# The triangular solve of a recurrent mixer in blocks of 8 with Horner steps, and decays as exponentials of scanned logarithms

## What is computed

```python
g = sigmoid(z @ g1) @ g2
kk = heads(k * k_k); kk = kk * rsqrt(sum(kk * kk) + 1e-12)
for d in range(2):                      # forward and backward in time
    w_log = -softplus(-(w0[d] + tanh(z @ w1[d]) @ w2[d])) - 0.5
    decay = exp(-exp(w_log))            # = exp(-exp(-0.5) * sigmoid(...))
    a = sigmoid(a0[d] + (z @ a1[d]) @ a2[d])
    kd = heads(k * (1 + (a - 1) * k_a))
    # scan over the 256 positions, one 64x64 state per head:
    #   sa    = state @ (-kk_t)
    #   state = state * decay_t + sa (x) (kk_t * a_t) + v_t (x) kd_t
    #   y_t   = state @ r_t
```

## Time and profile before

| | us |
|---|---|
| median of 3 runs | 3765.77 (3765.65 to 3765.84) |
| the profiled execution, its own time | 3762.42 |
| its span, from the first to the last instruction | 3760.6 |

### The profile page before, as it was taken

One profiled execution on the slowest core, in us unless ns is written; L12 is line 12 of the kernel. 1 busy time (PEld: TensorE's weight loads), 2 busy tenths in 40 slices (PEclk: granted clock), 3 DMA queues, 4 the chain that ended last, 5 costly groups with the idle time before them and its releaser, 6 DMA issues. The chain is left out here.

```text
span 3760.6 us, 63506 instructions
## 1 busy us (share of the span) xinstructions
PE 3675.8 (98%) x26848; PEld 3401.5 (90%) x26848; DVE 2378.3 (63%) x4235; ACT 424.9 (11%) x1010; POOL 1169.8 (31%) x926
## 2 busy tenths in 40 slices
PE   7999999999999999999989999999999999999998
PEld 6778885999999999999977888859999999999998
DVE  7986853894688654444389867539946885444442
ACT  1014211100111000000010232111101110000000
POOL 3610000033333355554245100001333334554552
PEclk9999999999999999999999999999999999999999
DMA  5440113599999999999653401146999999999995
GB/s 167 143 136 23 35 58 118 203 398 409 392 388 405 378 364 362 361 358 371 227 158 123 133 29 35 53 127 226 393 413 385 394 408 380 373 369 359 353 364 205
DMA packets 312536, 994.17 MB, mean 264 GB/s; under 512 B 59341, under 2 KB 170317, under 8 KB 231053
## 3 DMA queue, kind: packets, MB, share of 16 engines
q0 software_dynamic: 118944, 587.71, 40.5%
q1 hardware_dynamic: 193312, 402.41, 29.1%
HBM read 1071.38 MB, written 2.10 MB: 285 GB/s over the span
## 5 line engine op out<-in xcount | busy, mean ns | idle before, releaser
L1840 PE MATMUL bank<-ycT,ex_tile 128*128 128x160 f32 x8192 | 1130.5, 299 | 0.0
L1840 PEld LDWEIGHTS bank<-ycT,ex_tile 128*128 128x128 f32 x8192 | 1115.8, 190 | 7.0 <-issue 6.7
L1913 PEld LDWEIGHTS bank<-ex_W,ex_tile 128*128 128x128 f32 x8192 | 1113.3, 190 | 6.8 <-issue 6.7
L1913 PE MATMUL bank<-ex_W,ex_tile 128*128 128x160 f32 x8192 | 1116.6, 299 | 0.0
L1779 POOL DMA_INDIRECT ex_row<-in_peer_u,ex_rows x244 | 256.8, 1052 | 1529.3 <-DVE ex_rows L2073 1062.1
L2115 DVE CUSTOM_DVE_ANT_0 ex_row<-ex_row,ex_h_wide 128x2048 f32<-128x2048 f32 x192 | 439.1, 2290 | 355.3 <-DMA ex_row<-in_peer_u,ex_rows 353.9
L2121 DVE SCALAR_TENSOR_TENSOR ex_sums<-ex_row,ex_weight,ex_sums 128x2048 f32<-128x2048 f32 x186 | 437.3, 2351 | 349.7 <-DMA ex_row<-in_peer_v,ex_rows 349.4
L1790 POOL DMA_INDIRECT ex_tile<-in_peer_v,ex_wanted x256 | 314.1, 1227 | 486.6 <-PE bank L1913 435.7
L459 PE MATMUL pj_bank<-pj_hT,pj_piece 128*128 128x256 f32 x2048 | 454.6, 382 | 4.4 <-DVE pj_hT L813 4.4
L459 PEld LDWEIGHTS pj_bank<-pj_hT,pj_piece 128*128 128x128 f32 x2048 | 387.3, 190 | 70.2 <-issue 13.7
L1779 POOL DMA_INDIRECT ex_row<-in_peer_v,ex_rows x128 | 125.6, 981 | 247.7 <-DVE ex_sums L2121 187.8
(11 more groups left out here) (395 smaller groups left out, 3460.9 us busy)
## 6 DMA issues: line engine op xcount, KB each, us to landing
ex_tile<-in_peer_uT SPq DMA_DIRECT2D x256, 1024.0 KB, 8.1
pj_piece<-in_w_in SPq DMA_DIRECT2D x32, 2048.0 KB, 8.5
arena<-in_w_out SPq DMA_DIRECT2D x20, 1024.0 KB, 5.1
query_w<-in_peer_w_query SPq DMA_DIRECT2D x16, 1024.0 KB, 6.0
rw_low_rank<-in_w_out SPq DMA_DIRECT2D x12, 512.0 KB, 4.1
ex_row<-in_peer_u,ex_rows POOLq DMA_INDIRECT x314, 9.6
ex_row<-in_peer_v,ex_rows POOLq DMA_INDIRECT x256, 8.8
ex_tile<-in_peer_v,ex_wanted POOLq DMA_INDIRECT x256, 7.9
```

The lines of the kernel that those rows point to most:

```text
L1840: mm = mmul(o, ring[:, j % SLOTS, k * P:k * P + P], hT[k // 4][:, k % 4, 0:DENSE], start=(k == 0), stop=(k == KT - 1))
L1913: mm = mmul(bank[:, at_, lo:lo + DENSE], ring[:, i % SLOTS, m * P:m * P + P], W[:, j, :], start=(j == 0 and m % 3 == 0), stop=(j == TILES ...
```

## The change

The blocks of the solve become 8 positions instead of 16. Inside them the inverse I + N + ... + N^7 is formed as W3 = I + NT + N2T, then twice W <- W3 + N3·W (`h1`, `h2`), with N3 = N2·N. Across the blocks M = W·No is formed, and X <- X0 + M·X is done three times (`y1`, `y2`, `y3`), starting from X0 = W·R. That is nn, n2, n3 (its product is the one behind `h1`), h1's product (behind `h2`), two after `h2` (`x`, `m`), and one behind each of `y1` to `y3`: nine products of two directions. `NTo` is no longer masked out of the first product; `No` is masked out of the transposed one next to `N`. The squares' copies on ACT become fewer, and the adds on DVE become more.

`fill(3i)` is cut in two halves, one before and one after `h1`'s product. On DVE, `prepare_1` is split: the shifts of r and k stay before the first add, kk comes between `h1` and `h2` with the new `prepare_sums` and the shift of v. `prepare_3` comes before `y1`. `prepare_decays` is gone: DVE scans the sigmoids as sums (`prepare_sums`), and ACT makes the decays, their reciprocals, the shifted and the end values from the sums by six Exp (`exponents`) at the end of its part of a group, followed by a Sqrt of one column. DVE waits for them (`decay_out`) before `prepare_pairs`. The Exp over all decays in `mixers` is gone, and that stage makes the first group's `exponents` and `prepare_sums`.

```diff
-    parts["m16U"], parts["m16L"] = s16 & (q > p), s16 & (q < p)
-    parts["mXU"], parts["mXL"] = s32 & ~s16 & (q > p), s32 & ~s16 & (q < p)
+    parts["m8U"], parts["m8L"] = s8 & (q > p), s8 & (q < p)
+    parts["mXU"], parts["mXL"] = s32 & ~s8 & (q > p), s32 & ~s8 & (q < p)
...
+def prepare_sums(nc, do, first, i, ready):
+    V, dec, inside, Pc = nc.vector, decay(first, i), first["D1"], first["Pc"]
     for d in range(2):
         o = slice(None, None, -1) if d else slice(None)
-        do(V.tensor_tensor_scan(Pc[:, d, o], dec[:, d, o], D1[:, d, o], 0.0, ALU.mult, ALU.add), wait=(d == 1))
-    do(V.reciprocal(first["IP"][:], Pc[:]), wait=False)
-    do(V.tensor_copy(n32(Pe[:, 0, :])[:, :, 1:], n32(Pc[:, 0, :])[:, :, :-1]), wait=False)
...
+        do(V.tensor_tensor_scan(Pc[:, d, o], inside[:, d, o], dec[:, d, o], 0.0, ALU.mult, ALU.add), ready if d else None,
+           wait=False)
+def exponents(nc, do, first, ready):
+    A, Pc, Pe, pend = nc.scalar, first["Pc"], first["Pe"], first["pend"]
+    n32 = lambda a: a.rearrange("p (n s) -> p n s", s=CH)
+    do(A.activation(first["IP"][:], Pc[:], ACT.Exp, scale=LOG_DECAY), wait=False)
+    do(A.activation(n32(Pe[:, 0, :])[:, :, 1:], n32(Pc[:, 0, :])[:, :, :-1], ACT.Exp, scale=-LOG_DECAY), wait=False)
+    do(A.activation(n32(Pe[:, 1, :])[:, :, :-1], n32(Pc[:, 1, :])[:, :, 1:], ACT.Exp, scale=-LOG_DECAY), wait=False)
+    do(A.activation(pend[:, 0, :], Pc[:, 0, CH - 1::CH], ACT.Exp, scale=-LOG_DECAY), wait=False)
+    do(A.activation(pend[:, 1, :], Pc[:, 1, 0::CH], ACT.Exp, scale=-LOG_DECAY))
+    do(A.activation(Pc[:], Pc[:], ACT.Exp, scale=-LOG_DECAY), ready, wait=False)
...  PE, one group
                 for d in range(2):
                     dve(f"nn{d}")
-                    product(d, 2 + 2 * d, mats["N"], mats["NT"])
-                    ev(product(d, 3 + 2 * d, mats["NT"], mats["N"]))
+                    ev(product(d, 2 + 2 * d, mats["N"], mats["NT"]))
...
                 for d in range(2):
-                    act(f"sq2{d}")
-                    product(d, 2 * d, mats["N2"], mats["N2T"])
-                    ev(product(d, 2 * d + 1, mats["N2T"], mats["N2"]))
+                    act(f"n2{d}")
+                    ev(product(d, 3 + 2 * d, mats["N2T"], mats["N"]))
...
                 for d in range(2):
-                    ev(product(d, 4 + d, mats["N2"], mats["W"]))
-                fill(3 * i)
+                    act(f"n3{d}")
+                    dve(f"w3{d}")
+                    ev(product(d, 2 + 2 * d, mats["N3"], mats["W3"]))
+                fill(3 * i, [0])
                 for d in range(2):
-                    act(f"sq4{d}")
-                    dve(f"w2{d}")
-                    ev(product(d, d, mats["N4"], mats["W"]))
+                    dve(f"h1{d}")
+                    ev(product(d, 3 + 2 * d, mats["N3"], mats["W6"]))
                 if not last:
                     act("trK")
                     head_sums(i + 1, 0)
+                fill(3 * i, [1])
                 for d in range(2):
-                    ev(product(d, 2 + d, mats["N4T"], mats["N4"]))
+                    dve(f"h2{d}")
+                    ev(product(d, d, mats["W"], R))
+                    ev(product(d, 2 + 2 * d, mats["No"], mats["W"]))
                 for d in range(2):
-                    act(f"sq8{d}")
-                    dve(f"w4{d}")
-                    ev(product(d, 4 + d, mats["N8"], mats["W"]))
+                    act(f"m{d}")
+                    ev(product(d, 3 + 2 * d, mats["MT"], mats["X0"]))
                 for d in range(2):
-                    dve(f"w8{d}")
-                    ev(product(d, d, mats["W"], R))
+                    dve(f"y1{d}")
+                    ev(product(d, d, mats["MT"], mats["X1"]))
                 for d in range(2):
-                    act(f"x{d}")
-                    ev(product(d, 2 + d, mats["NTo"], R))
-                for d in range(2):
-                    act(f"no{d}")
-                    ev(product(d, 4 + d, mats["W"], Yo))
+                    dve(f"y2{d}")
+                    ev(product(d, 2 + 2 * d, mats["MT"], mats["X2"]))
                 if not last:
                     head_sums(i + 1, 1)
                 for d in range(2):
-                    dve(f"z{d}")
+                    dve(f"y3{d}")
...  ACT, behind the copies of x and m
+                if i < GT - 1:
+                    act.wait_ge(log_sums, i + 1)
+                    exponents(nc, do, first, decay_out)
+                    do(A.activation(first["kq2"][:, 0:1], c("eps"), ACT.Sqrt), wait=False)
...  DVE, one group
                         masked(d, b0, 1, "Rb", "m32" + w + "i", wait=False)
-                        masked(d, b0, 0, "NT", "m16" + w, wait=False)
-                        masked(d, b0, 0, "NTo", "mX" + w, dve_ev)
+                        masked(d, b0, 0, "NT", "m8" + w, dve_ev)
...
-                    do(V.tensor_tensor(eb(mats["N"], d), src, m4("m16" + "LU"[d]), ALU.mult), dve_ev, wait=(d == 1))
+                    do(V.tensor_tensor(eb(mats["N"], d), src, m4("m8" + "LU"[d]), ALU.mult), wait=False)
+                    do(V.tensor_tensor(eb(mats["No"], d), src, m4("mX" + "LU"[d]), ALU.mult), dve_ev, wait=(d == 1))
...
-                if more:
-                    prepare_1(i + 1)
-                    prepare_decays(nc, do, first, i + 1)
-                grow("w2")
-                grow("w4")
-                grow("w8")
+                for d in range(2):
+                    dve.wait_ge(act_ev, at(ACT_EV, i, f"n2{d}"))
+                    do(V.tensor_tensor(jk(mats["W3"], d), jk(mats["N2T"], d), jk(mats["W3"], d), ALU.add), dve_ev, wait=False)
+                if more:
+                    shift(sr[:], 0, i + 1)
+                    shift(sk[:], 1, i + 1)
...
+                add("h1", (2, 4), mats["W6"], mats["W3"])
+                if more:
+                    do(V.scalar_tensor_tensor(kq[:], sk[:], col("k_k", i + 1), sk[:], ALU.mult, ALU.mult))
+                    do(V.tensor_scalar(kq[:], kq[:], col("k_k", i + 1), None, ALU.mult), kq_ready)
+                    prepare_sums(nc, do, first, i + 1, log_sums)
+                    shift(sv[:], 2, i + 1)
+                add("h2", (3, 5), mats["W"], mats["W3"])
                 if i % 2:
                     add_unit((1, 4)[i // 2])
                 if more:
                     prepare_3(i + 1)
-                for d in range(2):
-                    pe(f"z{d}")
-                    do(V.tensor_tensor(jk(R, d), bank[:, 4 + d, :], jk(R, d), ALU.add), dve_ev, wait=False)
+                add("y1", (3, 5), mats["X1"], mats["X0"])
+                add("y2", (0, 1), mats["X2"], mats["X0"])
+                add("y3", (2, 4), R, mats["X0"])
                 if more:
+                    dve.wait_ge(decay_out, i + 1)
                     prepare_pairs(nc, do, first, i + 1)
```

More of the change, by code:

```diff
@@ L987, in _ @@
                 dve.wait_ge(decay_out, 1)
-                prepare_decays(nc, do, first, 0)
                 dve.wait_ge(unit_out, 34)
@@ L1375, in _ @@
                 for d in range(2):
[L1376 to L1378 removed]
+                    pe(f"n3{d}")
+                    do(A.copy(jk(mats["N3"], d), bank[:, 3 + 2 * d, :]), act_ev, wait=False)
                 pe("trK")
@@ L1382, in _ @@
                     kk_root(i + 1)
-                for name, dst, b0 in (("sq8", mats["N8"], 2), ("x", R, 0), ("no", Yo, 2)):
-                    for d in range(2):
-                        pe(f"{name}{d}")
-                        do(A.copy(jk(dst, d), bank[:, b0 + d, :]), act_ev, wait=False)
+                for d in range(2):
+                    pe(f"x{d}")
+                    do(A.copy(jk(mats["X0"], d), bank[:, d, :]), act_ev, wait=False)
+                    pe(f"m{d}")
+                    do(A.copy(jk(mats["MT"], d), bank[:, 2 + 2 * d, :]), act_ev, wait=False)
+                if i < GT - 1:
+                    act.wait_ge(log_sums, i + 1)
+                    exponents(nc, do, first, decay_out)
+                    do(A.activation(first["kq2"][:, 0:1], c("eps"), ACT.Sqrt), wait=False)
                 for d in range(2):
```

79 lines of the change are left out of this document (33 added, 46 removed).

## The result

The changed kernel takes 3720.89 us (median of four runs, 3718.04 to 3721.91) against 3765.71 for the kernel before beside it (3763.39 to 3765.84). The ratio is 0.9882, with a 95% interval of 0.987 to 0.9893: faster by 1.2%, 44.8 us by the medians. Forecast were 33.4 us and 3732.4; the range began at 3723.0, so the kernel is faster than the range allowed. The two profiled executions took 3762.42 and 3721.74, which is 40.7 apart. Two more measurements of the same kernel gave 3724.44 and 3725.2 beside 3765.37 and 3765.29, gains of 40.9 and 40.1. The interval of the first one is narrower than the kernels' own scatter, because its few runs happened to lie close together; single executions of the kernel before lie up to 9 us apart, and those of the changed kernel up to 10.

What follows compares the result with a forecast made beforehand. PE was taken to bound each group, with DVE having some 10 us to spare. Later groups 22.6, first groups 9.3 and the stage before 1.5 sum to 33.4 us: 3729.0, or 3732.4 for a median run; range 3723 to 3743.

Steps and rivals of the forecast that it cites:

- if the clock falls as before: First groups: PE's clock again drops to half, losing 3.4 us in the first layer and 4.1 in the second.
- Rival 1: The clock doesn't fall in one or both first groups: gain 40.9 us without falls (3724.9), 37 with one; chance 0.30.
- a median run: Whole kernel: the profiled execution lay 3.4 us below the runs' median, so 3729.0 became 3732.4.
- The waits before y1: Solve's middle: PE waits for DVE's first y1 add, 1.65 us in an odd group, 1.05 in an even one.
- The stage before: Ahead of the first group: PE's 0.73 us wait for the third square goes in both layers, 1.5 us.
- the wait of 0.32 before the second `gh`: Second group's end: PE's wait of 0.32 us, one of the two waits left out of the sum.
- a place where the clock doesn't fall: Recurrence: PE busy 2.44 of 3.40 us, without a fall of the clock.
- The price of a product: Solve, on PE: nine products at 1.80 us instead of eleven totalling 20.06, 3.85 us less in a group.
- the front: Group's start: DVE masks two tiles instead of three for `pa0`, PE gains 0.25 us, `trB` starts at 14.25, before 16.34.
- the hidden exponents: ACT's Exps, group's end: decay_out comes between 32 and 34.3 us, DVE asks at 36.0; counted as zero.
- the end of a chain without pauses is set by its whole length: DVE from W3 to y1: no pause, so the wait before y1 is the chain's length, 16.2 us.
- The rival in which waits lower the clock: Preparing groups: thinner PE work brings falls of 3.4 us at least; two per group make it 7.4 slower (3773); chance 0.05.

Runs made afterwards that it cites:

- before_covered: The kernel before with unused extra matmuls on PE in its two waits in the first group of each layer; 3757.25 us against 3764.98, ratio 0.998.
- change_third: The changed kernel as it is, measured once more with rounds and traced; 3725.2 us.
- shifts_earlier: The changed kernel with the shifts of r and k for the third and fourth groups moved into DVE's pauses ending the group before; 3719.75 us.
- solve_only: The changed kernel's new solve with the old decays put back, in the stage before too; 3765.98 us against 3764.98 for the kernel before, ratio 0.9999.

## Why the prediction was wrong in size

The account of the two traces, forecast and measured, in us over both layers:

| term | forecast | measured |
|---|---|---|
| first groups, from `trV` to `trV` | 9.3 | 17.5 (8.1 and 9.4); 17.1 by the means of all traces |
| second groups | 7.1 | 8.4 |
| third groups | 7.1 | 8.9 |
| fourth groups | 8.3 | 8.1 |
| stage before, recurrence and all the rest | 1.5 | -2.2 |
| sum | 33.4 | 40.7 |

**The step that failed is "if the clock falls as before".** It is the term of 3.4 and 4.1 us in the first groups. I wrote that the waits in the first groups would be 0.7 and 1.3, and they are 0.72 and 1.21. I gave 11.4 us from `trV` to `trB` at full clock; it is 11.6 (346.32 to 357.90). Then I added 3.4 and 4.1 us for a fall in both layers and called that the likeliest case. In the trace there was none, and over all traces of the changed kernel one first group in four had one. These 7.5 us are about the whole of the 7.3 between the two sums, 33.4 and 40.7. By their first groups without a fall (46.63 in `before_covered`, 41.60), 10.0 of the 17.5 us are the shorter front and the missing product, and 7.4 are falls that the traced kernel before had and the traced changed kernel had not. Rival 1 had this case, at 3724.9, with a chance of 0.30; its 40.9 us is what the two traces show. The evidence that I had named, that PE would be busy 1.4 to 1.7 us of 3.41 against 1.09, pointed that way, and I went by the old outcome instead. The fall of the old kernel was itself a cost of its waits (`before_covered`), so whatever shortened these had to put it in doubt. Why falls became rarer stays open, as the table above shows; that the traced execution had none at all is in part luck.

**A second term, for the other 4.2 us.** The forecast median is 11.5 us above the measured one, and the traces account for 7.3. I had put 3.4 us on top for "a median run", because the profiled execution of the kernel before was that much below its median. That offset belonged to one execution and not to the kernel: the profiled execution of the changed kernel lies 0.85 above its median, and three more traces of the kernel before took 3765.8 to 3767.2. Part of it is clock too: the first group of the first layer took 49.69 us in the traced execution and 50.95 to 51.25 in those three. And 3720.9 was a low median: over all 15 executions it is 3723.3.

**Smaller terms.** The waits before y1 are 0.42, 1.17 and 0.42 where I had 1.05, 1.65 and 1.05: the second W3 add ended 0.35 us earlier than I had it and the scans take 1.2, not 1.3, so y1 began 30.15 from the start instead of 30.6 (and my own two ends, 29.8 and 31.3, are 1.5 apart, not 1.65). And the wait of 0.32 before the second `gh`, which I left in, is gone: DVE starts `prepare_pairs` 0.28 us behind the start of `qy`, not 0.45. Together that is 3.1 us more than forecast in second and third groups. The stage before gave its 1.5 as forecast, PE's waits for the third square are gone, yet the row of the rest is -2.2. Some 2.5 us are two longer waits of PE for DVE's `pj_h` and `pj_hT` between the layers, in a stretch that varies by 4 us between executions of the changed kernel; no run ties them to the change. Another 1.9 went in the recurrence, where PE's unexplained waits (issue) were 3.7 us in both layers against 1.9 before:

```profile
L1327 PE MATMUL bank<-rw_QT,arena 64*64 64x32 f32 x512 | 17.8, 218 | 3.7 <-issue 3.7
```
```profile
L1320 PE MATMUL bank<-rw_QT,arena 64*64 64x32 f32 x512 | 17.5, 218 | 1.9 <-issue 1.9
```

This is hardly an accident of one trace. From its first matmul to the output projection the recurrence took 16.5 to 19.6 us in six of twelve cases in the six traces of the changed kernel, and 17.0 in one of eight in the four of the kernel before; all others took 15.0 to 15.5. The means are 16.5 and 15.4, a difference of 2.2 us an execution. With the variants it is 12 of 28 with the new solve against one of 12 with the old. Why the new solve should bring these waits more often, no run shows. The prediction also had the recurrence as a place where the clock doesn't fall. It did not in the stretch of the earlier trace rows, but it fell in the recurrence in eight of all twenty traces (one of the kernel before, two of the changed one, five of the variants), in or right behind issue waits of 1.3 to 1.9 us, while the one of 2.15 us in the profiled execution of the changed kernel brought none. A stretch of it in `change_third`:

```profile
2386.90:2393.70 6.80, 6.22 (x118) 6.21 (x118) 0.99 (x2) 0.00 (x0) 0.00 (x0) 0.50 0.01 3
```

**The range.** Its lower end stood 2 us under rival 1 and knew no spread of single executions. That spread is 3759.5 to 3768.5 for the kernel before and 3718.0 to 3728.0 for the changed one. The median of four runs came out at 3720.9, two others at 3724.4 and 3725.2, inside the range, and so is that of all executions, 3723.3. So how far the forecast missed is partly the luck of the few runs; that its likeliest case was 9 us too slow is not. A range for a median of few runs needs some 3 us more at either end here.

**What held.** The price of a product and its number (3.85 us a group), the front, the hidden exponents, the wait that moves to y1 (where "1 to 1.7 us in each preparing group" was too much: it is 0.42 in two of three) and its cause in DVE's order, and that all but 2 to 4 us of the gain carries through the later stages. That the end of a chain without pauses is set by its whole length did not hold: `shifts_earlier` took 2.9 us out of it and the wait stayed. The rival in which waits lower the clock had too small a place in my thinking; it did not come true in the solve of the changed kernel, but in its recurrence now and then, and `solve_only` shows it eating a whole change.

Open remains why the same waits bring a fall in one layer and not in the other, whether the stage ahead of them has a part in it, and what PE's issue waits are: they appear where the transfers of the output weights are dense (DMA share 1.04 in the recurrence), but nothing was tried on them.

## What to carry to other kernels

Look for stretches at the lower clock in the kernel before, and ask what PE did ahead of them: a change that shortens those waits may win back the clock as well, several times what it saves itself, so price both outcomes and don't take the old one as given. Where one engine's order of work is as long as the other's, the halves of a change can each be worth nothing and together everything; measure them together before dropping either. A wait at the end of a busy queue is shortened by what stands behind the last event that the queue itself waits for, not by anything ahead of it.

## What the runs showed of the hardware

The granted clock fell to 0.50 (1.2 GHz) behind waits of PE as short as 1.39 and 1.21 us within a few microseconds, in ten of twelve cases, and cost 3.05 us for a stretch of 6.83 us and 4.3 us in the mean of the kernel before. With waits of 0.72 and 1.21 it fell in six of 24, and with the waits covered in none of four. Behind one wait of 3.9 us it fell in the trace of `solve_only` in every preparing group of both layers; in the recurrence it fell in eight of 40, in or right behind issue waits of 1.3 to 1.9 us; behind single waits of 1.1 to 1.2 us in otherwise full stretches of the solve's second to fourth groups it fell in no trace. A change of table on ACT took 1.28 us in every trace, with the next Exp 0.01 us behind it and the load 0.02 us behind the copy before, where the Trainium skill ("ScalarE: Activation LUTs", section "What ACT_TABLE_LOAD costs") gives some 2.66 us for every switch, a drain included; the measurement decides. A 128x512 Exp took 0.63 us.
